# SSD mixer of an encoder kernel: accumulators emptied ahead of the weight splits, a new order at the mixer's two ends, its last two output units by token tile

## The chip, the cores and the metric

One core of one Trainium2 chip runs the whole kernel in one launch. The metric is the device time in microseconds (us). The kernel before takes 1647.73 us, the median of 3 runs (1646.65 to 1647.95).

## The reference

Four encoder layers on 256 tokens of width 1024, float32. Layers 0 and 3 have a bidirectional Mamba-2 mixer (SSD), layer 1 a gated short convolution, layer 2 a neighbourhood attention; a squared-ReLU MLP follows each, and each sub-layer ends in a layer norm. The SSD mixer:

```python
def ssd_mixer(x, w_in, conv_w, conv_b, dt_bias, a_log, d_skip, norm_w, w_out):
    zxbcdt = x @ w_in
    ...
    xbc = jax.nn.silu(depthwise_conv(xbc, conv_w) + conv_b)
    ...
    dt = jax.nn.softplus(dt_raw.reshape(bsz, seq, 2, SSD_HEADS) + dt_bias)
    y_fwd = run_ssd(xs, dt[:, :, 0], a_coef[0], bm, cm)
    y_bwd = flip(run_ssd(flip(xs), flip(dt[:, :, 1]), a_coef[1], flip(bm), flip(cm)))
    y = y_fwd + y_bwd + d_skip[:, None] * xs
    y = y.reshape(bsz, seq, SSD_D_INNER) * jax.nn.silu(z)
    return grouped_rmsnorm(y, norm_w) @ w_out
...
for i in range(DEPTH):
    ...
    x = layer_norm(alpha * x + h, ln_mix_g[i], ln_mix_b[i])
    x = layer_norm(alpha * x + sq_relu_mlp(x, ffn_w_in[i], ffn_w_out[i]), ln_ffn_g[i], ln_ffn_b[i])
```

`run_ssd` works in two chunks of 128 tokens: products within a chunk under a decay, and a state that one chunk passes to the other (the cross-chunk product).

## The kernel before

The weights come as units of 128 x 2048 float32 (1 MB). The list `units` (`plan_units`, L64) numbers them in the order of use. SyncE loads unit u into one of 3 buffers `raw` as soon as unit u-3 is split (L342). A split makes two fp32r halves: ScalarE writes `w_high` (L997), and then VectorE writes `w_low` = raw - w_high (L1338), into one of 4 slots. The slot is free when TensorE has used unit u-4 (semaphore `w_used`). TensorE multiplies three times per product (high by high, high by low, low by high).

Every engine runs its program in the order in which `build` issues it and waits on semaphores. Where a split stands in it is set by `split_to(u)`, which issues all splits up to unit u that are not issued yet. `result` is at L1000 on ScalarE and L1341 on VectorE:

```python
            def result(u):

                split_to(u + 3)
                act.wait_ge(w_used, u + 1)
                return acc_of[u]
```

So whoever empties the accumulator of unit u first splits unit u+3.

An SSD mixer has 8 groups g. Each has the units `z` (gate), `bc` (B and C), `x` and `so` (a slice of the output matrix); before them comes `dt`. The order of units is dt, z0, bc0, x0, z1, bc1, x1, z2, bc2, x2, so0, z3, bc3, x3, so1, ... z6, bc6, x6, so4, bc7, x7, z7, so5, so6, so7. TensorE's program for one step i (L848 to L858) is

- `project` z i (`tokens`, L570), then `state_products(i-1)` (L800, reads `bc` after its silu) and `turn_xs(i-1)` (L789, four transposes of `x` after its silu);
- `project` bc i (`features`, L557), `cross_chunk(i-1)` (L811) and `scan(i-1)` (L824);
- `project` x i (L557), `out_unit` so i-2 (L681, into the four banks `Y`), `turn_gated(i-1)` (L835, transposes of the gated and normalised output).

The products of L789, L800, L811, L824 and L835 share two PSUM banks `inner` in turn (`inner_bank`, L530): each waits until the one two places before it has been read. The bank of `turn_gated(g)` is read by ScalarE's `gated_high` (L1148) and then VectorE's `gated_low` (L1488), which write the operand `opT` of the output unit.

ScalarE and VectorE share the rest of a group. `start_conv` (L1062, L1068) copies the accumulator into a padded buffer and does the first tap, `taps` (L1468) on VectorE the other four; `conv_tanh` (L1076) and `silu_bc`, `silu_x`, `silu_z` (L1480) make the silu. `shift_decays` (L1091), `decays` (L1101), `join_decays` (L1498, a predicated copy) and `decayed_products` (L1508 to L1522) make the operand of `scan`. `copy_cross` (L1112) and `copy_xs` (L1121) empty the banks of L800 and L789. GpSimd scales the copied `x` twice (L432) and loads the next decays (L427). `add_cross` (L1532, L1537) and `gate_scan` (L1548, L1550) add up and gate; `squares` (L1130), a power on GpSimd (L459, L460) and `normalise` (L1138) make the grouped norm.

At the start of a mixer `time_constants` works on `dt`, and the cumulative sums go by TensorE (L771), a VectorE copy (L1594), TensorE again (`cumsum_rows`, L779) and DRAM. At its end `tail` (L699) does the last output unit by token tile, so that the layer norm of tile 0 (`norm`, L1356) can start while TensorE multiplies tile 1; the feed-forward begins with the transposes of L647 and three units of L570.

## Time and profile before

| | |
|---|---|
| profiled execution, its own time | 1646.52 us |
| its span | 1644.6 us |
| mean granted TensorE clock | 0.946 |
| TensorE matmul busy | 1491.3 us (91%) |
| TensorE weight load busy | 1379.9 us (84%) |
| VectorE busy | 991.2 us (60%) |
| ScalarE busy | 767.6 us (47%) |
| GpSimd busy | 163.9 us (10%) |
| chain that ended last | PE 66%, DVE 18%, issue 8%, ACT 7%, DMA 1% |
| DMA | 266.98 MB, mean 162 GB/s |

PE, PEld, DVE, ACT, POOL and SP are TensorE's matmuls, its weight loads, VectorE, ScalarE, GpSimd and SyncE. The granted clock is given as a share of full speed; the two levels are 0.50 (1.2 GHz) and 1.00 (2.4 GHz), and a mean between them is a share of time at each. The first mixer lies between 20 and 330 us, the second between 1142 and 1447 us. A row of the profile that reads "[4.20 <-DVE opT L1488]" says that the engine stood idle for 4.20 us before this instruction until the VectorE instruction of line 1488 on the tile opT had ended. Matmuls overlap in their records, so the time that one block takes is read from its start to the start of the next.

### The profile page before, as it was taken

The page shows a single profiled execution, that of the slowest core. Times are in us where ns is not written, and L with a number is a line of the kernel's source. Part 1 is how long each engine was busy: PE and PEld are TensorE (multiplying, and loading weights), DVE is VectorE, ACT ScalarE, POOL GpSimd, SP SyncE. Part 2 cuts the span into 40 slices and gives each one's busy share as a digit, 9 for nine tenths or more (in the row PEclk, how much of TensorE's full clock was granted, in tenths as well). Part 3 has the DMA queues.
Part 4 walks back from the last instruction along what each step waited for, and adds up shares of the span by engine and source line. Part 5 has one row for each costly group of instructions (what it writes and reads, how often), then busy time and mean ns, then how long its engine had stood idle before and what let it go on. Part 6 is the DMA issues. An engine that isn't in the chain of part 4 may idle for free.

```text
span 1644.6 us, 24792 instructions
## 1 busy us (share of the span) xinstructions
PE 1491.3 (91%) x9837; PEld 1379.9 (84%) x9837; DVE 991.2 (60%) x1227; ACT 767.6 (47%) x1103; POOL 163.9 (10%) x245
## 2 busy tenths in 40 slices
PE   6888887799999999999999999999878787799996
PEld 6877887599998999999899799998878787689995
DVE  4767766655456666555754465556776776665554
ACT  3666655344433434443355444433656664435441
POOL 1111110052231000000000000000111120000000
PEclk9899898899999999999999999999999988899998
DMA  7635543346674564555553345555644462336551
GB/s 220 183 126 154 172 138 127 102 147 200 207 218 156 188 210 143 187 195 205 170 171 121 102 138 183 194 203 151 190 152 132 152 179 103 122 110 205 205 179 52
DMA packets 198193, 266.98 MB, mean 162 GB/s; under 512 B 11768, under 2 KB 167824, under 8 KB 198080
## 3 DMA queue, kind: packets, MB, share of 16 engines
q1 hardware_dynamic: 188032, 237.53, 43.6%
q0 software_dynamic: 9200, 27.55, 6.3%
q8 instruction: 79, 1.29, 0.3%
q10 hardware_dynamic: 848, 0.32, 0.1%
q14 instruction: 34, 0.28, 0.1%
HBM read 264.19 MB, written 1.18 MB: 161 GB/s over the span
## 4 chain that ended last, share of the span: by engine, by line
PE 66%; DVE 18%; issue 8%; ACT 7%; DMA 1%; SPq 0%; DVEq 0%; POOL 0%; ACTq 0%
PE acc L557 31%; PE y L681 24%; DVE conv L1468 6%; DVE w_low L1338 6%; PE acc L570 4%; ACT w_high L997 3%; PE y L570 1%; PE inner L789 1%; DMA raw<-in_ssd_w_in 1%; PE inner L811 1%; DVE opT L1488 1%; DVE gate L1550 1%; DVE gate L1548 1%; DVE E L1532 1%; ACT square L1130 1%
## 5 line engine op out<-in xcount | busy, mean ns | idle before, releaser
L557 PE MATMUL acc<-xT,w_high 128*128 128x256 f32 (+1 forms) x3392 | 646.2, 292 | 2.7 <-DVE xT L1399 1.1
L1338 DVE TENSOR_TENSOR w_low<-raw,w_high 128x2048 fp32r<-128x2048 f32 (+1 forms) x226 | 513.1, 2275 | 175.3 <-ACT w_high L997 93.3
L557 PEld LDWEIGHTS acc<-xT,w_high 128*128 128x128 f32 x3392 | 557.3, 201 | 7.8 <-issue 3.5
L997 ACT ACTIVATE w_high<-raw 128x2048 fp32r<-128x2048 f32 (+1 forms) x226 | 428.1, 1898 | 204.5 <-PE y L681 75.4
L557 PE MATMUL acc<-xT,w_low 128*128 128x256 f32 (+1 forms) x1696 | 492.8, 291 | 0.0
L681 PE MATMUL y<-w_high,opT 128*128 128x512 f32 x1408 | 404.3, 397 | 7.9 <-DVE opT L1488 6.0
L557 PEld LDWEIGHTS acc<-xT,w_low 128*128 128x128 f32 x1696 | 339.9, 200 | 0.0
L681 PEld LDWEIGHTS y<-w_high,opT 128*128 128x128 f32 x1408 | 263.9, 191 | 61.4 <-issue 9.5
L681 PE MATMUL y<-w_low,opT 128*128 128x512 f32 x704 | 226.3, 396 | 0.0
L570 PE MATMUL acc<-w_high,xT 128*128 128x256 f32 (+1 forms) x960 | 188.5, 298 | 15.6 <-DVE xT L1399 9.3
L1354 DVE TENSOR_TENSOR opT<-conv,opT 128x512 fp32r<-128x512 f32 x56 | 39.0, 696 | 267.2 <-issue 236.6
L570 PEld LDWEIGHTS acc<-w_high,xT 128*128 128x128 f32 x960 | 160.3, 205 | 19.4 <-issue 16.0
L681 PEld LDWEIGHTS y<-w_low,opT 128*128 128x128 f32 x704 | 134.5, 191 | 29.0
L570 PE MATMUL acc<-w_low,xT 128*128 128x256 f32 (+1 forms) x480 | 141.5, 295 | 0.0
L1468 DVE SCALAR_TENSOR_TENSOR conv<-conv_pad,ssd_par,conv 128x256 f32<-128x256 f32 x256 | 104.1, 479 | 3.4 <-ACT conv L1068 3.4
L1037 ACT ACTIVATE conv<-acc 128x512 f32<-128x512 f32 x60 | 35.8, 597 | 149.3 <-PE acc L557 135.1
L409 POOL TENSOR_TENSOR small<-small,minus_half 128x1 f32<-128x1 f32 x16 | 15.9, 993 | 842.6 <-DVE small L1375 842.6
L570 PEld LDWEIGHTS acc<-w_low,xT 128*128 128x128 f32 x480 | 98.7, 206 | 0.0
L789 PE MATMUL inner<-ident,xsT 128*128 128x128 f32 x64 | 16.1, 400 | 81.0 <-DVE opT L1488 78.5
L789 PEld LDWEIGHTS inner<-ident,xsT 128*128 128x128 f32 x64 | 10.6, 202 | 87.1 <-issue 68.0
L1076 ACT ACTIVATE tanh<-conv 128x512 f32<-128x512 f32 x32 | 20.2, 631 | 135.4 <-DVE conv L1468 135.4
L1024 ACT ACTIVATE xT<-inner 128x512 fp32r<-128x512 f32 x32 | 18.1, 595 | 117.5 <-PE inner L647 117.1
(182 smaller groups left out, 1175.6 us busy)
## 6 DMA issues: line engine op xcount, KB each, us to landing
raw<-in_ffn_w_in SPq DMA_DIRECT2D x128, 512.0 KB, 4.6
raw<-in_ffn_w_out SPq DMA_DIRECT2D x128, 512.0 KB, 4.4
raw<-in_ssd_w_in SPq DMA_DIRECT2D x96, 512.0 KB, 5.1
E<-cumsum_dram POOLq DMA_DIRECT2D x32, 512.0 KB, 5.5
raw<-in_ssd_w_out SPq DMA_DIRECT2D x32, 512.0 KB, 5.8
raw<-in_sc_w_in SPq DMA_DIRECT2D x24, 512.0 KB, 4.6
raw<-in_na_w_qkv SPq DMA_DIRECT2D x24, 512.0 KB, 4.6
raw<-in_sc_w_out SPq DMA_DIRECT2D x8, 512.0 KB, 4.4
```

Of the source, the lines that this page charges most:

```text
L557: mm = nc.tensor.matmul(bank[:, c * SEQ:(c + 1) * SEQ][:, span], w[:, col:col + P], xT[:, k, low, span], start=(k == 0 and part == 0), sto ...
L570: mm = nc.tensor.matmul(bank[:, t * width:(t + 1) * width], xT[:, k, low, t * P:(t + 1) * P], w[:, k * width:(k + 1) * width], start=(k == ...
L681: mm = nc.tensor.matmul(Y[t][c][:, :], opT[:, o % ACTS, low, k, t * P:(t + 1) * P], w[:, k * D + c * 512:k * D + (c + 1) * 512], start=(fi ...
L789: mm = nc.tensor.transpose(bank[:, t * GW + c * P:t * GW + (c + 1) * P], xsT[:, m % 2, c, t * P:(t + 1) * P], ident[:, :])
L811: mm = nc.tensor.matmul(bank[:, t * GW:(t + 1) * GW], cross[m % 2][:, (1 - t) * P:(2 - t) * P], xs_end[:, (1 - t) * GW:(2 - t) * GW], star ...
L997: nc.scalar.activation(w_high[:, u % SPLIT, 0:k * c], raw[:, u % RAW, 0:k * c], ACT.Copy).then_inc(w_high_done, 1)
L1024: nc.scalar.activation(xT[:, 4 * half:4 * half + 4, 0, t * P:(t + 1) * P], bank[:, :].rearrange("p (k c) -> p k c", k=4), ACT.Copy).then_i ...
L1037: nc.scalar.activation(conv[:, o % 2, :, :], views(bank[:, :]), ACT.Relu).then_inc(relu_done, 1)
L1076: nc.scalar.activation(th[:, m % 2, :], src, ACT.Tanh, scale=scale).then_inc(tanh_done, 1)
L1338: V.tensor_tensor(w_low[:, u % SPLIT, 0:k * c], raw[:, u % RAW, 0:k * c], f(w_high[:, u % SPLIT, 0:k * c]), ALU.subtract).then_inc(w_low_d ...
L1354: V.tensor_tensor(low, src, high, ALU.subtract).then_inc(op_low, 1)
L1468: ins = V.scalar_tensor_tensor(out=y, in0=pad[:, c % 2, i, q:q + SEQ], scalar=tap(j, q, ct), in1=y, op0=ALU.mult, op1=ALU.add)
```

## The change

It keeps every instruction and moves many. On ScalarE and VectorE the mixer no longer uses `result` but `finished`, which only waits for the accumulator; the split of unit u+4 is issued by an explicit `split_to` after the accumulator of unit u has been emptied and, in a step, after the short work that others wait for. In the first step `turn_gated(0)` moves behind the projection of z 2. The last step runs bc 7, x 7, z 7 in another order against the scans; `turn_gated(6)`, the halves of so 5 and the transposes change places; and so 6 and so 7 are done together by `tail`, token tile 0 of both and then tile 1 of both.

```diff
@@ TensorE
-            def tail(s, us, first=False):
+            def tail(s, us, first=False, between=None):
...
                             mm = out_part(s, u, o + i, first and i == 0, False, [t])
+                            if between and t == 0:
+                                between()
...
-                    for i in range(1, G):
-                        if i < G - 1:
-                            project(names[("z", i)], range(NT))
+                    for i in range(1, G - 1):
+                        project(names[("z", i)], range(NT))
+                        if i == 2:
+                            turn_gated(0)
                         state_products(i - 1)
                         turn_xs(i - 1)
                         project(names[("bc", i)], range(NT))
                         cross_chunk(i - 1)
                         scan(i - 1)
                         project(names[("x", i)], range(NT))
-                        if i < G - 1:
-                            if i >= 2:
-                                out_unit(s, names[("so", i - 2)], first=(i == 2))
+                        if i >= 2:
+                            out_unit(s, names[("so", i - 2)], first=(i == 2))
                             turn_gated(i - 1)
+                    project(names[("bc", G - 1)], range(NT))
+                    state_products(G - 2)
+                    turn_xs(G - 2)
+                    project(names[("x", G - 1)], range(NT))
+                    cross_chunk(G - 2)
+                    scan(G - 2)
                     project(names[("z", G - 1)], range(NT))
-                    turn_gated(G - 2)
                     state_products(G - 1)
+                    turn_xs(G - 1)
...
                     out_part(s, names[("so", G - 3)], o, False, False, [0])
-                    turn_xs(G - 1)
-                    out_part(s, names[("so", G - 3)], o, False, False, [1]).then_inc(w_used, 1)
+                    turn_gated(G - 2)
                     cross_chunk(G - 1)
                     scan(G - 1)
-                    out_unit(s, names[("so", G - 2)], between=lambda: turn_gated(G - 1))
-                    tail(s, [names[("so", G - 1)]])
+                    out_part(s, names[("so", G - 3)], o, False, False, [1]).then_inc(w_used, 1)
+                    tail(s, [names[("so", G - 2)], names[("so", G - 1)]], between=lambda: turn_gated(G - 1))
@@ ScalarE (VectorE the same)
+            def finished(u):
                 act.wait_ge(w_used, u + 1)
                 return acc_of[u]
+
+            def result(u):
+
+                split_to(u + 3)
+                return finished(u)
@@ ScalarE, the mixer
+                    split_to(names[("dt", 0)] + 4)
                     z_tanh(0)
-
-                    split_to(names[("bc", 0)] + 3)
...
                     act.dma_start(rows_dram[j], csT[:, :]).then_inc(rows_stored, 16)
+                    split_to(names[("z", 0)] + 4)
                     conv_tanh()
+                    split_to(names[("bc", 0)] + 4)
                     start_conv("x", 0)
+                    split_to(names[("x", 0)] + 4)
                     conv_tanh()
                     shift_decays(0)
                     for i in range(1, G):
...
+                            if i == 2:
+                                gated_high(0)
+                        else:
+                            start_conv("bc", i)
+                            split_to(names[("bc", i)] + 4)
                         copy_cross(i - 1)
                         copy_xs(i - 1)
+                        if i < G - 1:
+                            split_to(names[("z", i)] + 4)
                         shift_decays(i)
-                        start_conv("bc", i)
-                        conv_tanh()
+                        if i < G - 1:
+                            start_conv("bc", i)
+                            split_to(names[("bc", i)] + 4)
+                            conv_tanh()
+                        else:
+                            conv_tanh()
+                            start_conv("x", i)
                         squares(i - 1)
                         decays(i, early)
                         normalise(i - 1)
-                        start_conv("x", i)
+                        if i < G - 1:
+                            start_conv("x", i)
                         decays(i, late)
+                        split_to(names[("x", i)] + 4)
                         conv_tanh()
-                        split_to(names[("x", i)] + 4)
                         if i == G - 1:
-                            z_tanh(G - 1)
-                        gated_high(i - 1)
-                    copy_cross(G - 1)
-                    copy_xs(G - 1)
-                    split_to(names[("so", G - 1)] + 1)
+                            z_tanh(i)
+                            copy_cross(i)
+                            copy_xs(i)
+                            split_to(names[("z", i)] + 4)
+                        if i >= 2:
+                            gated_high(i - 1)
+                            split_to(names[("so", i - 2)] + 4)
                     squares(G - 1)
                     normalise(G - 1)
-                    split_to(names[("so", G - 1)] + 2)
                     gated_high(G - 1)
@@ VectorE, taps
-                        split_to(names[(kind, g)] + 3)
@@ VectorE, the mixer
+                    split_to(names[("dt", 0)] + 4)
                     silu_z(0)
-                    split_to(names[("bc", 0)] + 3)
...
+                    split_to(names[("z", 0)] + 4)
                     silu_bc(0, taps("bc", 0))
-                    silu_x(0, taps("x", 0))
+                    split_to(names[("bc", 0)] + 4)
+                    y = taps("x", 0)
+                    split_to(names[("x", 0)] + 4)
+                    silu_x(0, y)
...
+                            if i == 2:
+                                gated_low(0)
+                            decayed_products(i - 1)
+                            split_to(names[("z", i)] + 4)
+                            join_decays(i)
+                            add_cross(i - 1)
+                            y = taps("bc", i)
+                            gate_scan(i - 1)
+                            silu_bc(i, y)
+                            split_to(names[("bc", i)] + 4)
+                        else:
+                            y = taps("bc", i)
+                            decayed_products(i - 1)
+                            split_to(names[("bc", i)] + 4)
+                            silu_bc(i, y)
+                            join_decays(i)
+                            add_cross(i - 1)
+                            gate_scan(i - 1)
                         silu_x(i, taps("x", i))
-                        split_to(names[("x", i)] + 4)
                         if i == G - 1:
-                            silu_z(G - 1)
-                        gated_low(i - 1)
-                    decayed_products(G - 1)
-                    split_to(names[("so", G - 1)] + 1)
+                            silu_z(i)
+                            split_to(names[("x", i)] + 4)
+                            decayed_products(i)
+                            split_to(names[("z", i)] + 4)
+                        if i >= 2:
+                            gated_low(i - 1)
+                            if i < G - 1:
+                                split_to(names[("x", i)] + 4)
+                            split_to(names[("so", i - 2)] + 4)
+                        else:
+                            split_to(names[("x", i)] + 4)
                     add_cross(G - 1)
                     gate_scan(G - 1)
-                    split_to(names[("so", G - 1)] + 2)
                     gated_low(G - 1)
```

VectorE in a steady step of the kernel before (w_low is a split, opT<-inner the row of `gated_low`, the three rows of L1480 `silu_bc`, `silu_x` and `silu_z`):

```order
L1480 SCALAR_TENSOR_TENSOR ring_a<-tanh,conv 128x512
L1338 TENSOR_TENSOR w_low<-raw,w_high 128x2048
L1468 SCALAR_TENSOR_TENSOR conv<-conv_pad,ssd_par,conv 128x256 x8
L1480 SCALAR_TENSOR_TENSOR xsT<-tanh,conv 128x512
L1338 TENSOR_TENSOR w_low<-raw,w_high 128x2048
L1488 SCALAR_TENSOR_TENSOR opT<-inner,ssd_par,opT 128x256 x2
L1338 TENSOR_TENSOR w_low<-raw,w_high 128x2048
L1480 SCALAR_TENSOR_TENSOR ring_c<-tanh,acc 128x512
```

and of the change (the same lines are now L1508, L1364, L1496 and L1516):

```order
L1508 SCALAR_TENSOR_TENSOR ring_a<-tanh,conv 128x512
L1364 TENSOR_TENSOR w_low<-raw,w_high 128x2048
L1496 SCALAR_TENSOR_TENSOR conv<-conv_pad,ssd_par,conv 128x256 x8
L1508 SCALAR_TENSOR_TENSOR xsT<-tanh,conv 128x512
L1516 SCALAR_TENSOR_TENSOR opT<-inner,ssd_par,opT 128x256 x2
L1364 TENSOR_TENSOR w_low<-raw,w_high 128x2048 x2
L1508 SCALAR_TENSOR_TENSOR ring_c<-tanh,acc 128x512
```

The split of the next `x` unit moved from ahead of `gated_low` to behind it.

VectorE at the start of a mixer in the kernel before, from the copy of the cumulative sums' rows (L1603) to `silu_x(0)`:

```order
L1603 COPY cumsum_rows<-inner 64x256
L1468 SCALAR_TENSOR_TENSOR conv<-conv_pad,ssd_par,conv 128x256 x8
L1480 SCALAR_TENSOR_TENSOR ring_a<-tanh,conv 128x512
L1338 TENSOR_TENSOR w_low<-raw,w_high 128x2048
L1468 SCALAR_TENSOR_TENSOR conv<-conv_pad,ssd_par,conv 128x256 x8
L1480 SCALAR_TENSOR_TENSOR xsT<-tanh,conv 128x512
```

and of the change:

```order
L1631 COPY cumsum_rows<-inner 64x256
L1364 TENSOR_TENSOR w_low<-raw,w_high 128x2048
L1496 SCALAR_TENSOR_TENSOR conv<-conv_pad,ssd_par,conv 128x256 x8
L1508 SCALAR_TENSOR_TENSOR ring_a<-tanh,conv 128x512
L1364 TENSOR_TENSOR w_low<-raw,w_high 128x2048
L1496 SCALAR_TENSOR_TENSOR conv<-conv_pad,ssd_par,conv 128x256 x8
L1364 TENSOR_TENSOR w_low<-raw,w_high 128x2048
L1508 SCALAR_TENSOR_TENSOR xsT<-tanh,conv 128x512
```

Three splits stand in this stretch where one stood: the first came from ahead of the sums, the last from behind `silu_x(0)`.

VectorE at the end of a mixer of the change, from `silu_z(7)` (ring_c) to `gated_low(7)`, the last row:

```order
L1508 SCALAR_TENSOR_TENSOR ring_c<-tanh,acc 128x512
L1364 TENSOR_TENSOR w_low<-raw,w_high 128x2048
L1536 TENSOR_TENSOR E<-E,inner 128x1024
L1540 SCALAR_TENSOR_TENSOR E,small<-inner,ident 128x128 x2
L1550 SCALAR_TENSOR_TENSOR own_token<-dts,small,skip 128x4 x2
L1364 TENSOR_TENSOR w_low<-raw,w_high 128x2048
L1516 SCALAR_TENSOR_TENSOR opT<-inner,ssd_par,opT 128x256 x2
L1364 TENSOR_TENSOR w_low<-raw,w_high 128x2048
L1560 TENSOR_TENSOR E<-inner,decay_from_end 128x512
L1565 TENSOR_TENSOR E<-E,ring_b 128x512
L1576 TENSOR_TENSOR gate<-E,inner 128x512
L1578 SCALAR_TENSOR_TENSOR gate<-gate,ring_c 128x512
```

The three splits are so 7 and the feed-forward's units 0 and 1. Before, unit 0 stood there too, ahead of `add_cross(7)`, and unit 1 between `gate_scan(7)` and `gated_low(7)`; now unit 1 stands ahead of `add_cross(7)`.

## Rows read from the trace of the kernel before

**Rows 1.** TensorE's waits, second mixer: waited for, us in total, times, longest

```profile
PE inner L789 <- DVE opT L1488: 38.5, 7, 9.9
PE inner L835 <- ACT gate L1138: 5.3, 2, 4.9
PE inner L779 <- DVE cumsum L1594: 3.3, 1, 3.3
```

**Rows 2.** Stretches: length, busy of PE, PEld, DVE, ACT, POOL, clock, DMA share, GB/s

```profile
1222.61:1358.35 135.74, 118.93 (x803) 112.75 (x802) 95.83 (x148) 81.07 (x156) 21.12 (x24) 0.90 0.51 156
106.33:242.17 135.84, 119.06 (x803) 112.89 (x802) 95.73 (x148) 81.06 (x156) 21.13 (x24) 0.90 0.51 155
1248.65:1252.65 4.00, 4.00 (x21) 4.00 (x20) 3.93 (x10) 3.62 (x10) 1.16 (x1) 0.50 1.10 305
```

**Rows 3.** Timeline around one wait of L789: start us, us, engine, line, operation

```profile
1276.44 1.89 ACT L997 ACTIVATE w_high<-raw 128x2048 fp32r<-128x2048 f32 x1
1276.65 0.69 DVE L1480 SCALAR_TENSOR_TENSOR xsT<-tanh,conv 128x512 f32<-128x512 f32 x1 [0.77 <-ACT tanh L1076]
1278.24 0.82 ACT L1148 ACTIVATE opT<-inner,ssd_par 128x256 fp32r<-128x256 f32 x2
1278.43 2.29 DVE L1338 TENSOR_TENSOR w_low<-raw,w_high 128x2048 fp32r<-128x2048 f32 x1 [1.09 <-ACT w_high L997]
1280.63 0.87 DVE L1488 SCALAR_TENSOR_TENSOR opT<-inner,ssd_par,opT 128x256 fp32r<-128x256 f32 x2
1281.65 1.08 PE L789 MATMUL inner<-ident,xsT 128*128 128x128 f32 x4 [4.20 <-DVE opT L1488]
```

**Rows 4.** Timeline of TensorE, block starts in the same step

```profile
1290.28 0.60 PE L811 MATMUL inner<-ring_a,E 128*128 128x256 f32 x2
1292.85 0.48 PE L557 MATMUL acc<-xT,w_high 128*128 128x256 f32 x2
1298.68 0.63 PE L681 MATMUL y<-w_high,opT 128*128 128x512 f32 x2
1304.15 0.60 PE L835 MATMUL inner<-ident,gate 128*128 128x128 f32 x4
```

**Rows 5.** Groups of lines in steady steps: xcount | busy us, mean ns | idle before

```profile
L1338 DVE TENSOR_TENSOR w_low<-raw,w_high 128x2048 fp32r<-128x2048 f32 x16 | 36.6, 2288 | 21.4 <-issue 17.0 <-ACT w_high L997 4.3
L1498 DVE COPY_PREDICATED E<-suffix,E 128x1024 f32<-128x1024 uint32 x4 | 5.4, 1356 | 0.0
L1508 DVE TENSOR_TENSOR E<-E,inner 128x1024 f32<-128x1024 f32 x4 | 4.9, 1215 | 0.0
L432 POOL TENSOR_TENSOR ring_b<-ring_b,own_token 128x512 f32<-128x512 f32 x1 | 2.1, 2052 | 1.8 <-DVE own_token L1522 1.8
L432 POOL TENSOR_TENSOR ring_a<-ring_b,decay_to_end 128x512 f32<-128x512 f32 x8 | 8.8, 1101 | 125.6 <-ACT ring_b L1121 111.3 <-issue 14.3
```

**Rows 6.** Timeline of the start of the second mixer

```profile
1161.83 2.29 DVE L1338 TENSOR_TENSOR w_low<-raw,w_high 128x2048 fp32r<-128x2048 f32 x1 [0.82 <-issue]
1165.38 0.58 ACT L1062 ACTIVATE conv_pad<-acc 128x512 f32<-128x512 f32 x1
1166.49 0.58 ACT L1068 ACTIVATE conv<-conv_pad,ssd_par 128x256 f32<-128x256 f32 x1
1167.11 3.26 DVE L1468 SCALAR_TENSOR_TENSOR conv<-conv_pad,ssd_par,conv 128x256 f32<-128x256 f32 x8 [1.65 <-ACT conv L1068]
1179.91 0.66 PE L789 MATMUL inner<-ident,xsT 128*128 128x128 f32 x4 [1.34 <-DVE xsT L1480]
```

**Rows 7.** Timeline of the end of the second mixer

```profile
1427.59 0.69 DVE L1550 SCALAR_TENSOR_TENSOR gate<-gate,ring_c 128x512 f32<-128x512 f32 x1
1430.31 0.91 ACT L1138 ACTIVATE gate<-gate,small 128x256 f32<-128x256 f32 x2 [1.09 <-POOL small L460]
1446.99 0.47 PE L570 MATMUL acc<-w_high,xT 128*128 128x256 f32 x2 [0.84 <-DVE xT L1399]
```

**Rows 8.** DMA issues of the page: count, KB each, us to landing

```profile
raw<-in_ssd_w_in SPq DMA_DIRECT2D x96, 512.0 KB, 5.1
```

28 lines of the change are left out of this document (12 added, 16 removed).

## The prediction

> **What bounds the kernel now.** I read the waits of TensorE first, then stretches with granted clock, then the timelines of the places where it waits. Outside the two SSD mixers TensorE has hardly a gap. Inside the second mixer its largest wait is one line's: the transposes of `turn_xs` (L789) wait seven times, 38.5 us in all, for a VectorE row of L1488, `gated_low`; behind it come `turn_gated` (L835) and `cumsum_rows` (L779) [rows 1]. The steady part of a mixer, four steps from the cross-chunk product of group 1 to that of group 5, takes 135.74 us in the second mixer and 135.84 in the first, 34.0 a step, at a mean granted clock of 0.90 [rows 2]. So the clock is at its lower level, 1.2 GHz, part of the time: the four microseconds after one of these waits show 0.50 [rows 2].
>
> One wait in detail [rows 3]. The bank that `turn_xs` wants is the one that held the turned gate of the group before, and it comes free when `gated_low` (L1488) ends, 1281.50. That row stands behind a weight split: ScalarE splits at 1276.44 before it copies the turned gate at 1278.24, VectorE's w_low runs from 1278.43, then L1488. TensorE has nothing to do for 4.20 us. What follows is slow too: the four transposes and the `bc` projection behind them take 8.63, from 1281.65 to the next product at 1290.28; at full clock the equal `x` projection takes 5.83, and four transposes 0.4 [rows 3, 4].
>
> **The change, part by part.** No instruction is added or removed, matmuls and splits are as many; only their order changes, so each term is a shift of waits.
>
> *A steady step (groups 1 to 5).* `gated_high` and `gated_low` now run before the split of the next `x` unit instead of behind it. If TensorE never waits, a step costs the 34.0 less the wait (4.2, and 0.2 by which the next matmul overlaps the last) and less what the lower clock adds (8.63 - 6.23 = 2.4): 27.2. Does VectorE keep up? It is busy 95.83/4 = 23.96 of a step [rows 2]. I laid its chain out from the start of a cross-chunk product, with w_low at 2.2 since successive VectorE rows overlap by 0.08: `add_cross`, two 128x512 rows of 0.69, starts at 1.06 and ends at 2.45; four taps of two tiles (3.26 [rows 6]) 5.65; `gate_scan` 7.0; from its end to the end of the normalised gate 2.94 [rows 7], 9.95; pad and first tap on ScalarE 1.69 [rows 6], 11.65; taps 14.9; tanh 0.65, 15.55; `gated_high` 0.82, 16.4; `gated_low` 0.87, 17.2 [rows 3]; two w_low (2.29 [rows 5]) 21.6; `silu_z` 22.2; products 1.2 [rows 5] and small rows 0.9, 24.3; w_low 26.5; the predicated copy 1.36 [rows 5], 27.8. The next `add_cross` can start at 28.2. So the chain fits, 0.4 to spare, and what TensorE waits for (L1488 at 17.2, wanted near 21) has 4 us in hand. TensorE is the bound, at full clock: 4 x (34.0 - 27.2) = **27.2 a mixer**. The loads: 5.3 MB a step now in 27.2, 195 GB/s after 156 [rows 2]; each is issued when w_low three units earlier ends, 5.1 from issue to landing [rows 8], and in my layout each has over 4 us left.
>
> *The mixer's start* (second mixer's times). w_low of `bc` 1, which held up the cumulative sums until 1164.12 [rows 6], moves behind them: the copy of the sums is 3.0 earlier, the 3.3 wait of L779 goes [rows 1]. But three splits now stand between the sums and `silu_x(0)`, where one stood, and VectorE's w_low waits each time for ScalarE's w_high (1.89 [rows 3]), which has moved behind the pad: pad and first tap of `bc` 0 end at 1164.1, w_high 1166.0, w_low 1168.3, taps 1171.5, tanh 1172.1, w_high 1174.0, pad and tap of `x` 0 1175.7, w_low before it 1176.4, taps 1179.6, w_low of `z` 2 1181.8, `silu_x` 1182.5. `turn_xs(0)` ran at 1179.91 after 1.34 of waiting [rows 6]; now at 1182.5, after 8.2, and the clock falls: `bc` 1 ends 5.2 later than before. Then `z` 2 fills the 4.9 that `turn_gated(0)` waited [rows 1], so `z` 2 ends 4.0 earlier. The split of `so` 0 still stands ahead of `gated_low(0)`; `turn_xs(1)` runs at 1212.2, was 1214.9. At the cross-chunk product of group 1 the gain is **2.3 a mixer**, nearly nothing for so much moved.
>
> *The mixer's end*, from the cross-chunk product of group 5 (its start is 0 here). Before, the feed-forward's first matmul came at 1446.99 - 1358.35 = 88.64 [rows 2, 7]. Now `bc` 7 and `x` 7 come ahead of the work that waited 9.9. VectorE: taps of `bc` 7 end 25.2, products 27.3, w_low 29.5, `silu_bc` 30.1, predicated copy 31.5, `add_cross` 32.9, gate 34.15, taps of `x` 7 37.4; ScalarE normalises until 37.1, decays 38.4, splits `so` 7 until 40.25, tanh 40.9; `turn_xs(7)` runs at 41.6, TensorE was there at 36.5: a wait of 5.1. Half of `so` 5 at half clock until 47.4, `turn_gated(6)` 48.0. `scan(7)` wants the bank that `gated_low(6)` empties behind w_low of the feed-forward's unit 0: 49.8 to 51.6. The second half of `so` 5 ends 54.4 and only then can its slot be split again (the feed-forward's unit 1), which both engines do **ahead of** `add_cross(7)` and `squares(7)`: w_high 56.3, w_low 58.7, `add_cross` 60.1, gate 61.4, normalised 64.3 [rows 7]. TensorE has the first half of `so` 6 until 57 and then waits 7.3 for `turn_gated(7)`, 1.9 more for L1488. Three halves follow (5.47/2 each at full clock [rows 4], 8.2, and 2.1 for the clock): 77.2. The last two units by token tile cover the layer norm of tile 0, whose 1.2 wait goes; the feed-forward starts at 79.4. Gain 88.64 - 79.4 = **9.2 a mixer**.
>
> Sum: 2 x (27.2 + 2.3 + 9.2) = 77.4. From the profiled 1646.5 that gives 1569.1; the median of the runs is 1.2 higher, **1570**.
>
> *The rule that speaks against it.* GpSimd's two products of L432 have the same shape; the one on ring_a takes 1101 ns, the one on ring_b in a steady step 2052, while VectorE's w_low stays at its 2288 in the mean of sixteen [rows 5]. So where they meet it is GpSimd that is held, and it has time. In the new order L432 falls beside a w_low, a row with two SBUF inputs. The Trainium skill (SBUF — State Buffer, SBUF: two separate sides) says that VectorE with two SBUF inputs and a GpSimd operation exclude each other for a whole instruction, whichever starts first. By the rule VectorE could as well be the one that stands still; this trace shows GpSimd's side of it, 2052 against 1101, and not VectorE's. What the other side would make here is rival A.
>
> **Rivals.** *A: VectorE becomes the bound.* Two L432 in its chain, 1.1 and 1.0, make the chain 27.8 - 1.06 + 2.1 = 28.9 a step, over TensorE's 27.2 by 1.7. Four steps lose 7, of which TensorE's 4 in hand cover more than half, and the end starts late: 4 to 7 a mixer, 1578 to 1584. For it: 88% busy, 0.4 to spare. Against: w_low never differs by a GpSimd row's length in this trace.
> *B: the wait is only shortened.* ScalarE or a bank I placed too early leaves 1 to 2 us before L789, and the clock still falls after each: a step saves 3, not 6.8, 30 less in all: 1600. Against: 4 us in hand.
> *C: slower, the loads.* The splits of `x` and `so` are now back to back, so loads are issued in bursts. If two of four loads of each step landed a load's 5.1 [rows 8] late on VectorE's chain, a step would take 37.4, 3.4 over now, 27 for eight steps; less the 23 won at both ends: 1651. It decides once a step loses over 9.7. Against: 4 us of room at the tightest.
> *D: nothing changes.* The split could have been no cause, another bank release being as late: 1647. Against: [rows 3] show w_low alone between the copy and L1488.
> The start and end may also miss: if `turn_xs(0)` or the end of the mixer were no better than now, 2.3 + 9.2 a mixer fall away, 1593; if VectorE and ScalarE hide the long waits there, each wait is worth 5 to 7, 1556.
>
> **How the numbers follow.** Forecast 0.70, A 0.14, B 0.11, C 0.02, D 0.03. The range takes A and the misses at the ends, from 1556 to 1593; B, C and D stay out. About 0.2% is what a measurement of this kernel tells from no change. Faster 0.96, same 0.02, slower 0.02.
>
> **What would show it.** Right: 108 to 110 us between the cross-chunk products of groups 1 and 5 at granted clock 1.00, no L789 wait in the steady steps; two waits of 5 to 9 us left at the start (L789), one of 5 before `turn_xs(7)` and one of 7 before `turn_gated(7)`. Wrong: VectorE without gaps in the steady steps and its `add_cross` later after each product (A); L789 still waiting (B); w_high waiting for raw (C).

## The result, and the profile after

The changed kernel takes 1594.41 us, the median of 4 runs (1592.47 to 1595.0), beside 1647.76 for the kernel before (1646.65 to 1647.95): a ratio of 0.9676, 95% interval 0.9659 to 0.9692. The forecast was 1570 with a range up to 1593. The profiled run took 1592.47 with a span of 1590.6, so 54.0 of span went where 77.4 were forecast.

TensorE's waits in the second mixer, answering to [rows 1] (line, what it waited for: us in all, times, longest):

```profile
PE inner L791 <- DVE xsT L1508: 10.9, 2, 8.1
PE inner L837 <- ACT gate L1148: 10.2, 4, 7.5
PE inner L791 <- DVE opT L1516: 7.4, 1, 7.4
PE inner L813 <- DVE E L1540: 4.4, 4, 3.6
```

L789 is now L791 and L1488 is L1516. The seven waits of 38.5 us for `gated_low` have become one, at the start. The steady steps have no L791 wait, as forecast. The waits for the normalised gate (L837 on L1148) have grown from 5.3 us to 10.2, and waits for a bank that VectorE empties late (L813) are new.

Four steps from the product of group 1 to that of group 5, in the first mixer and in the second, and last the end of the second mixer up to the feed-forward's first matmul (us, busy time of PE, PEld, DVE, ACT, POOL, granted clock, DMA share, GB/s), answering to [rows 2]:

```profile
104.81:217.27 112.46, 109.91 (x802) 103.17 (x801) 93.99 (x145) 81.56 (x157) 34.86 (x23) 1.00 0.55 175
1194.69:1307.17 112.48, 109.89 (x803) 103.16 (x801) 94.02 (x145) 81.49 (x157) 34.82 (x23) 1.00 0.55 177
1307.17:1394.17 87.00, 67.45 (x385) 59.50 (x385) 59.86 (x93) 39.87 (x79) 18.76 (x14) 0.86 0.36 122
```

The clock is up, at 1.00. But 112.5 is not the 108.8 of the forecast: the four steps of the second mixer are 27.12, 27.45, 28.95 and 28.96. And the end takes 87.00, hardly less than the 88.64 before, where 79.4 was forecast.

One late step on GpSimd, ScalarE and VectorE shows where the time goes (start us, us, engine, line):

```profile
1278.54 3.03 POOL L432 TENSOR_TENSOR ring_b<-ring_b,own_token 128x512 f32<-128x512 f32 x1 [1.84 <-DVE own_token L1550]
1281.51 1.15 POOL L427 DMA_DIRECT2D E<-cumsum_dram  x2
1289.59 1.82 POOL L459 TENSOR_SCALAR small<-small 128x2 f32<-128x2 f32 x1 [6.92 <-ACT square L1140]
1291.49 0.71 POOL L460 TENSOR_TENSOR small<-small,minus_half 128x2 f32<-128x2 f32 x1
```

```profile
1292.23 0.91 ACT L1148 ACTIVATE gate<-gate,small 128x256 f32<-128x256 f32 x2 [1.57 <-POOL small L460]
```

```profile
1278.37 2.29 DVE L1364 TENSOR_TENSOR w_low<-raw,w_high 128x2048 fp32r<-128x2048 f32 x1
1280.58 2.19 DVE L1526 COPY_PREDICATED E<-suffix,E 128x1024 f32<-128x1024 uint32 x1
...
1287.86 0.69 DVE L1578 SCALAR_TENSOR_TENSOR gate<-gate,ring_c 128x512 f32<-128x512 f32 x1
1288.47 0.69 DVE L1508 SCALAR_TENSOR_TENSOR ring_a<-tanh,conv 128x512 f32<-128x512 f32 x1
1289.07 2.28 DVE L1364 TENSOR_TENSOR w_low<-raw,w_high 128x2048 fp32r<-128x2048 f32 x1
1294.79 3.26 DVE L1496 SCALAR_TENSOR_TENSOR conv<-conv_pad,ssd_par,conv 128x256 f32<-128x256 f32 x8 [3.43 <-ACT conv L1078]
```

L459 works on 128x2 elements and still takes 1.82 us: it ends at 1291.41, when w_low (L1364) has ended at 1291.35. ScalarE's normalise (L1148) waits for it and ends at 1293.14, 4.59 after the gate (L1578 ended at 1288.55), not 2.94; the pads of `x` follow, and VectorE idles 3.43 before its taps. L432 begins under a w_low and ends at 1281.57, 0.99 after VectorE has started its next row, the predicated copy (L1526). That row stands still meanwhile: it takes 2.19 us, where it took 1356 ns in the mean [rows 5]. As groups over the four steps (xcount | busy us, mean ns), after, and below them L459 of the kernel before in its own four steps:

```profile
L1526 DVE COPY_PREDICATED E<-suffix,E 128x1024 f32<-128x1024 uint32 x3 | 6.6, 2188 | 0.0
...
L432 POOL TENSOR_TENSOR ring_a<-ring_b,decay_to_end 128x512 f32<-128x512 f32 x4 | 11.1, 2778 | 42.7 <-ACT ring_b L1131 42.7
L432 POOL TENSOR_TENSOR ring_b<-ring_b,own_token 128x512 f32<-128x512 f32 x3 | 9.1, 3026 | 5.5 <-DVE own_token L1550 5.5
L459 POOL TENSOR_SCALAR small<-small 128x2 f32<-128x2 f32 x4 | 7.3, 1817 | 23.3 <-ACT square L1140 23.3
```

```profile
L459 POOL TENSOR_SCALAR small<-small 128x2 f32<-128x2 f32 x4 | 0.8, 193 | 24.0 <-ACT square L1130 24.0
```

Nothing was added to GpSimd. Its busy time in four steps grew from 21.12 us to 34.82 [rows 2], and the rows that grew are those that meet a w_low.

### The profile page after: what moved, and what is told of

It is laid out like the page before. It is cut to its first block, busy times and chain, and to the rows that moved or that the text cites. A ratio compares the mean times of both kernels' runs of the same rounds, so it can differ in the third digit from the quotient of the medians.

```text
span 1590.6 us, 24788 instructions
## 1 busy us (share of the span) xinstructions
PE 1470.5 (92%) x9837; PEld 1357.3 (85%) x9837; DVE 997.9 (63%) x1227; ACT 769.1 (48%) x1103; POOL 212.5 (13%) x245
## 4 chain that ended last, share of the span: by engine, by line
PE 63%; DVE 21%; ACT 7%; issue 6%; POOL 2%; DMA 1%; SPq 0%; DVEq 0%; ACTq 0%; POOLq 0%
PE acc L557 28%; PE y L681 26%; DVE w_low L1364 6%; DVE conv L1496 6%; PE acc L570 4%; ACT w_high L1004 2%; POOL small L459 1%; DVE E L1526 1%; ACT square L1140 1%; PE y L570 1%; DVE E L1536 1%; DMA raw<-in_ssd_w_in 1%; POOL small L460 1%; DVE gate L1578 1%; DVE E L1565 1%
## 5 line engine op out<-in xcount | busy, mean ns | idle before, releaser
L557 PE MATMUL acc<-xT,w_high 128*128 128x256 f32 (+1 forms) x3392 | 625.2, 286 | 2.7 <-DVE xT L1428 1.1
L1364 DVE TENSOR_TENSOR w_low<-raw,w_high 128x2048 fp32r<-128x2048 f32 (+1 forms) x226 | 514.5, 2284 | 110.1 <-ACT w_high L1004 82.0
L557 PEld LDWEIGHTS acc<-xT,w_high 128*128 128x128 f32 x3392 | 538.8, 195 | 7.8 <-issue 3.5
L557 PE MATMUL acc<-xT,w_low 128*128 128x256 f32 (+1 forms) x1696 | 483.5, 285 | 0.0
L557 PEld LDWEIGHTS acc<-xT,w_low 128*128 128x128 f32 x1696 | 329.5, 194 | 0.0
L1496 DVE SCALAR_TENSOR_TENSOR conv<-conv_pad,ssd_par,conv 128x256 f32<-128x256 f32 x256 | 105.7, 485 | 41.2 <-ACT conv L1078 41.2
L432 POOL TENSOR_TENSOR ring_a<-ring_b,decay_to_end 128x512 f32<-128x512 f32 x16 | 33.2, 2075 | 187.7 <-ACT ring_b L1131 169.0
L496 POOL DMA_DIRECT2D E<-in_na_rpb x64 | 34.1, 538 | 92.4 <-ACT conv L1047 91.3
```

Source lines behind the costliest of these rows:

```text
L432: return nc.gpsimd.tensor_tensor(spread(dst, shape), spread(tri_b[:, n % 2, :], shape), factors, ALU.mult)
L496: pool.dma_start(dst, src).then_inc(window_landed[h % WINDOW_BUFS], 16)
L557: mm = nc.tensor.matmul(bank[:, c * SEQ:(c + 1) * SEQ][:, span], w[:, col:col + P], xT[:, k, low, span], start=(k == 0 and part == 0), sto ...
L1364: V.tensor_tensor(w_low[:, u % SPLIT, 0:k * c], raw[:, u % RAW, 0:k * c], f(w_high[:, u % SPLIT, 0:k * c]), ALU.subtract).then_inc(w_low_d ...
L1496: ins = V.scalar_tensor_tensor(out=y, in0=pad[:, c % 2, i, q:q + SEQ], scalar=tap(j, q, ct), in1=y, op0=ALU.mult, op1=ALU.add)
```

## The experiments

All times below are medians, with the ratio to the kernel before run beside them. The stretches are read from one profiled run of each kernel, from the first matmul of each cross-chunk product and of the feed-forward (us, first mixer / second mixer). "between" is from the feed-forward behind the first mixer to group 0's product of the second, so it holds the start of the second mixer too:

```text
kernel              group 0-1      groups 1-5       5 to feed-fwd   between  span
before              34.91/34.37    135.84/135.74    88.67/88.64     857.4    1644.6
changed             32.61/31.14    112.46/112.48    86.75/87.00     859.5    1590.6
e1 mean square      28.58/30.21    108.48/108.48    80.38/81.37     868.5    1578.1
e2 own sliver       31.10/31.16    109.93/109.97    87.02/84.88     859.8    1583.7
e3 both             30.18/28.69    108.48/108.48    80.21/79.69     858.6    1562.5
e4 undo x+4         33.32/31.80    120.14/118.74    84.82/85.73     859.7    1605.4
e9 undo bc+4        33.09/31.60    116.85/115.80    88.32/89.71     859.8    1607.1
e13 undo both       33.77/33.74    121.97/123.45    87.36/87.25     868.4    1627.3
e14 undo z+4 too    33.78/34.32    135.35/136.08    87.69/87.72     868.3    1654.5
e5 start            30.48/30.37    112.48/112.45    88.69/86.97     854.0    1581.0
e6 end              32.61/31.16    112.51/112.45    76.09/79.10     859.7    1574.3
e7 late turn        28.93/27.88    109.71/109.68    82.37/81.95     859.6    1570.4
e8 all three        27.98/27.07    113.13/113.14    74.66/74.66     853.7    1548.4
e11 late and end    27.60/27.73    109.72/109.68    73.08/71.47     861.4    1552.5
```

### Is it GpSimd? (e1, e2, e3)

e1 moves the scale of the mean square from GpSimd to VectorE, with a reciprocal in place of the power, so it leaves out that part of the output:

```diff
                             silu_bc(i, y)
+                            rms(i - 1)
                             split_to(names[("bc", i)] + 4)
 ...
-                        rms_power(g)
```

> GpSimd's two small operations per group (the scale 1/sqrt of the mean square) are done by VectorE behind silu_bc instead, and GpSimd's are dropped; the power is replaced by a reciprocal, so this part of the output is not computed. Theory 1 (GpSimd's small operation waits for the end of w_low, 1.82 us instead of 0.19, and so delays normalise, the pads of x, and VectorE itself): the steady step falls from 28.95 us to about 27.3, PE's wait ahead of turn_gated (0.9) goes, the idle time of VectorE ahead of taps x falls from 3.4 to about 1.7, total about 1594 - 2 x 5.5 x 1.6 = 1576 us. Theory 2 (VectorE's own work with ScalarE's chain is 29 us long and GpSimd's stretch is only a by-product with slack): step 28.9, total 1592 to 1597.

Measured: 1577.53 us (1575.76 to 1579.8), ratio 0.9576 [0.956, 0.9592]. Four steps with the end behind them, second mixer:

```profile
1191.77:1300.25 108.48, 108.48 (x803) 103.40 (x802) 98.19 (x156) 81.82 (x156) 20.18 (x16) 1.00 0.61 189
1300.25:1381.62 81.37, 64.15 (x387) 56.83 (x385) 57.34 (x96) 39.85 (x79) 12.11 (x8) 0.87 0.36 118
```

Every step is 27.12 and TensorE is busy for all of 108.48; VectorE is busier than before (98.19 after 94.02) and yet in time. The end is 5.6 shorter too (6.4 in the first mixer): it starts in time, and it is rid of an L459 of 1.82 of its own. That the median fits the expected number so well is partly luck: the mixers and what lies ahead of them gave 21.5 of span, and "between" took 9.0 more (see the last group).

e2 leaves GpSimd's second product a sliver of two columns:

```diff
-                        times_heads(xs_own, n, spread(own_token[:, n % 2, 0, :],
-                                                      [[HPG, NT], [1, HPG], [0, HD]])).then_inc(xs_skip, 1)
+                            nc.gpsimd.tensor_tensor(xs_own[:, 0:2], tri_b[:, n % 2, 0:2],
+                                                    own_token[:, n % 2, 0, 0:2], ALU.mult).then_inc(xs_skip, 1)
```

> GpSimd's product ring_b (1.04 us of its own) is shrunk to a sliver in groups 1 to 7, so the token's own term is left out there. Theory 1 (each of GpSimd's operations excludes VectorE's sbuf-to-sbuf ones): COPY_PREDICATED returns from 2.19 us to 1.36 and the step is 0.8 us shorter (28.1), total about 1585. Theory 2 (predicated copy is slow for another reason, its operands or ScalarE): it stays at 2.2 and the total at 1594.

Measured: 1585.88 us (1584.69 to 1597.39), ratio 0.9646 [0.9612, 0.968]; the last full steps are 28.14. VectorE's predicated copy in the four steps:

```profile
L1530 DVE COPY_PREDICATED E<-suffix,E 128x1024 f32<-128x1024 uint32 x3 | 4.0, 1349 | 0.0
```

It is back at 1349 ns with unchanged operands: what held it was L432.

> Both edits of the two kernels before. Theory 1: VectorE is rid of GpSimd save for one product a group, and PE sets the step, 27.1 us, as was forecast for the change; total about 1572. Theory 2: 1592 to 1597.

Measured: 1567.96 us (1564.21 to 1569.38), ratio 0.9518 [0.9503, 0.9533]. With both collisions away the stretches are what the forecast had: 108.48 for four steps (forecast 108.8), 80.21 and 79.69 for the end (forecast 79.4). Theory 2 fell in all three.

### What gave the 23 us of a mixer's steps? (e4, e9, e13, e14)

The prediction named one move, the gated operand ahead of the split of x+4. e4 takes that back (VectorE; ScalarE's tanh goes ahead of the split again as well):

```diff
-                            gated_low(i - 1)
-                            if i < G - 1:
-                                split_to(names[("x", i)] + 4)
+                        split_to(names[("x", i)] + 4)
+                        if i >= 2:
+                            gated_low(i - 1)
```

> Only the order in steps 2 to 6 (and the last) is taken back: the split x+4 stands ahead of the gated operand on both engines, everything else as changed. If this one move makes the shorter step, the step returns to about 33.9 us and the total to about 1594 + 2 x 4.5 x 4.9 = 1638. If the rest of the change (accumulators emptied before splits) gives half of it, the step is 31 and the total about 1615.

Measured: 1607.33 us (1604.38 to 1607.43), ratio 0.9756 [0.9742, 0.9771]. Both numbers were missed: four steps cost 7.7 and 6.3 more, not 20. The L791 waits are back in the second mixer's four steps, but with 8.0 us in all, the longest 2.8. e9 puts w_high of bc+4 back on ScalarE between normalise and the pads of `x`:

```diff
                             start_conv("bc", i)
-                            split_to(names[("bc", i)] + 4)
                             conv_tanh()
 ...
+                            split_to(names[("bc", i)] + 4)
                             start_conv("x", i)
```

> The changed kernel with one thing taken back on ScalarE alone: in steps 1 to 6 w_high of the unit bc+4 is made where it was before, between normalise and the pads of x, instead of ahead of the tanh of bc. VectorE's order is untouched. Theory 1 (the chain gate, normalise, pads of x, taps x sets the changed step, so what is put in it costs its full length): w_high's 1.9 us is added, step 28.95 to about 30.8, and the total 1594 + 2 x 5.5 x 1.9 less what the first steps have in hand, about 1610. Theory 2 (the chain has slack, since VectorE waits for GpSimd elsewhere anyway): 1594 to 1598.

Measured: 1608.51 us (1607.31 to 1609.52), ratio 0.9751 [0.9716, 0.9786]. Four steps 4.4 and 3.3 longer, the end 1.6 and 2.7: theory 1's total, though the late steps went to 29.8 and 30.9 unevenly.

> The changed kernel with the x+4 split ahead of the gated operand again (both engines) and w_high of bc+4 between normalise and the pads of x again (ScalarE). Theory 1 (the parts have separate prices that add, 13 and 14 us): 1621. Theory 2 (each is covered in part by what the others leave: whichever wait is removed, the next split in the chain takes its place, so only together do they give the whole): 1630 or more, steps of 32 to 34 us.

Measured: 1628.85 us (1628.5 to 1629.54), ratio 0.9876 [0.9846, 0.9906]. The median lies by theory 2's number, the stretches speak for theory 1: four steps cost 9.5 and 11.0 more than in the changed kernel, where the separate prices add to 12.1 and 9.6. The rest of the median is "between", 8.8 longer. e14 also puts the split of z+4 back (VectorE; ScalarE's goes back behind `shift_decays`):

```diff
-                            split_to(names[("z", i)] + 4)
                             join_decays(i)
                             add_cross(i - 1)
+                            split_to(names[("z", i)] + 4)
```

> As the kernel before, and the split of z+4 back behind shift_decays on ScalarE and behind add_cross on VectorE: a step's order as before, the ends as changed. Theory: steps 2 to 6 take 33.9 to 34.1 us again and the total is 1647 less what the ends gave, 4 to 8 us: 1639 to 1643. If a step stays below 33 something else in the change (PE's order, the so split) has a share that I haven't named.

Measured: 1655.71 us (1653.84 to 1657.33, 10 runs), ratio 1.0039 [1.0023, 1.0054]. The steps are back at 34.0 with four L791 waits of 4.19, as before. So of the 23 us of a mixer's four steps in the second mixer, the x+4 order carries 6.3, bc+4 with it 11.0, and z+4 the other 12.6, taken back in this order; z+4 was not taken back alone. The expected total was missed by 13: slower than the kernel before, although its steps are within 0.5 of before's and its ends (87.7) 0.9 shorter. The table puts the difference in "between": 868.3, where the kernel before has 857.4 and the changed one 859.5.

### Mending what was found (e7, e6, e5, e8, e11, e12, e15)

e7 leaves GpSimd alone, but takes what is urgent from behind it: TensorE turns the gated operand in the middle of the next z unit, and ScalarE makes the pads of `x` before it normalises.

```diff
-                        project(names[("z", i)], range(NT))
+                        zb = project(names[("z", i)], [0])
+                        if i >= 2:
+                            turn_gated(i - 2)
+                        project(names[("z", i)], [1], zb)
 ...
                         decays(i, early)
-                        normalise(i - 1)
                         if i < G - 1:
                             start_conv("x", i)
+                        normalise(i - 1)
```

> The changed kernel, whole computation, GpSimd's work left as it is, but nothing urgent hangs on it any more: the gated operand is turned in the middle of the next z projection, and ScalarE makes x's pads before it normalises. Theory 1 (GpSimd's blocked operation costs only because pads of x and turn_gated stand behind normalise): the step falls from 28.95 us to 27.1 to 27.5 though GpSimd's small operation stays long (1.8 us or more), total about 1578. Rival (the exclusion slows VectorE itself, which has no slack whatever the order): step 28.1 or more, total 1585 or more.

Measured: 1573.72 us (1572.3 to 1575.32), ratio 0.9555 [0.9539, 0.9571]. Steps of 27.42, and L459 is as slow as ever:

```profile
L459 POOL TENSOR_SCALAR small<-small 128x2 f32<-128x2 f32 x4 | 7.3, 1818 | 15.2 <-ACT square L1143 15.2
L432 POOL TENSOR_TENSOR ring_b<-ring_b,own_token 128x512 f32<-128x512 f32 x4 | 4.2, 1046 | 0.9 <-DVE own_token L1555 0.9
```

L459's collision stays, and TensorE waits for nothing in these steps (busy for 109.19 of 109.68); they are 0.3 each over e1's 27.12. But L432 no longer meets a w_low, which the edit brought along unasked: it takes 1.05, and the predicated copy 1.31. So e7 shows that L459's collision can be hidden, not that both can, and it doesn't tell the late turn from the early pads. It fits theory 1 in the step and is 4 better than its total.

e6 is about the wait of 7.5 before `turn_gated(7)`. Here are ScalarE and VectorE ahead of it in the changed kernel:

```profile
1369.26 1.92 ACT L1004 ACTIVATE w_high<-raw 128x2048 fp32r<-128x2048 f32 x1 [8.18 <-PE y L681]
```

```profile
1371.26 2.29 DVE L1364 TENSOR_TENSOR w_low<-raw,w_high 128x2048 fp32r<-128x2048 f32 x1 [8.61 <-ACT w_high L1004]
1373.47 0.68 DVE L1560 TENSOR_TENSOR E<-inner,decay_from_end 128x512 f32<-128x512 f32 x1
```

Both engines idle over 8 us because a split for the feed-forward waits for TensorE to be done with a slot, and `add_cross(7)` (L1560) is queued behind. The edit (VectorE the same):

```diff
-                        if i >= 2:
+                        if 2 <= i < G - 1:
                             split_to(names[("so", i - 2)] + 4)
```

> The changed kernel, whole computation, without the split of the feed-forward layer's first unit in the last step (it is made behind gated_low(7) then). Theory 1 (the wait of 7.5 us before turn_gated(7) is this split, which waits for PE to be done with output unit 5 and holds add_cross(7) and gate_scan(7) on VectorE behind it): the wait falls to 0 to 1 us, total about 1594 - 2 x 7 = 1580. Theory 2 (the wait is the length of the chain scan, gate, mean square, normalise, as the prediction held): it stays at 7 or more, total 1592 to 1595, or more if the split is then late for the next layer.

Measured: 1575.99 us (1574.16 to 1576.89), ratio 0.9565 [0.955, 0.9579]. The wait is gone and the end stretches are 10.7 and 7.9 shorter. The stretch of the second mixer:

```profile
1298.73:1377.83 79.10, 66.98 (x384) 59.32 (x385) 59.79 (x93) 39.76 (x79) 18.77 (x14) 0.89 0.39 134
```

e5 orders the start anew (ScalarE, then VectorE; what is moved leaves its old place, and ScalarE's `gated_high(0)` goes ahead of z 2 too):

```diff
                     z_tanh(0)
+                    split_to(names[("z", 0)] + 4)
 ...
-                    y = taps("x", 0)
-                    split_to(names[("x", 0)] + 4)
-                    silu_x(0, y)
+                    silu_x(0, taps("x", 0))
 ...
+                            if i == 2:
+                                gated_low(0)
                             silu_z(i)
+                            if i <= 2:
+                                split_to(names[("x", i - 1)] + 4)
```

> The changed kernel, whole computation, with the mixer's start ordered anew. ScalarE makes w_high(z0+4) right behind z_tanh(0), in time it idles; VectorE makes w_low(x0+4) and w_low(x1+4) behind silu_z of the next step, and both engines serve the gated operand of group 0 ahead of z 2. Theory 1 (the waits before turn_xs(0) and turn_xs(1) come from weight splits that stand ahead of the taps, of silu_x and of gated_low(0), not from VectorE's amount of work): the first wait falls from 8.1 us to about 5.6, the second from 7.4 to about 4, so 4 to 6 us a mixer, total 1582 to 1586. Theory 2 (VectorE has so much to do between bc 0 and x 1 that only the place of the wait moves): sum of the two waits stays within 1 us, total 1592 to 1595.

Measured: 1589.79 us (1582.93 to 1591.15), ratio 0.9641 [0.9619, 0.9663]. In the profiled run the two waits of TensorE in the second mixer are 3.1 and 5.8 instead of 8.1 and 7.4, 6.6 less together, as theory 1 has it, and the span is 9.6 less. But 3.0 of that lie ahead of group 0's product of the first mixer, where two executions of the changed kernel itself differ by 2.5 (72.20 and 74.70, the second from e16), and this execution is the lowest of four. The median, 4.6 less, lies between the two theories; e18 below repeats it.

> The three edits of the kernels before together, whole computation. If their parts add: 1594 less about 16 (late turn), 10 (start) and 14 (end) = about 1554 us. If the shorter start and the late turn gain the same waits: 1562.

Measured: 1550.38 us (1546.74 to 1553.24), ratio 0.9409 [0.9393, 0.9425]. The parts add: by their medians e7, e6 and e5 gave 20.7, 18.4 and 4.6, which makes 1550.7. Repeated on another chip:

> The kernel with the late turn, the mended start and the mended end, once more, in five rounds: 1547 to 1553 us, 0.941 of the kernel before.

Measured: 1557.31 us (1545.6 to 1563.4), ratio 0.9434 [0.9401, 0.9467]: above the expected range, with the mixers' stretches the same to 0.1 us and 863.8 between them in the profiled run. By either median it is faster than e5, e6 and e7. Without the start's edit:

> The late turn and the mended end together, start as changed. If the start is worth in this company what its two waits promise (5 to 7 us a mixer less), this kernel is 10 to 13 us above the one with all three edits, 1560 to 1563; if the start's gain only moves, 1552 to 1555.

Measured: 1553.09 us (1551.46 to 1564.94), ratio 0.9431 [0.9383, 0.948]. Not told apart from e8 and e15. The stretches show why so little is left: at group 1's product of the first mixer e8 is 7.2 ahead (95.56 after 102.77), e15, the same kernel, 4.1 (98.68). Then both give 3.4 back in the steps (113.13 after 109.72) and 1.6 at the end (74.66 after 73.08); in the second mixer the end gives back 3.2. I take it that VectorE still has the w_low rows to do that were put off; no run separates that. What is left of the start's gain in this company is not told from nothing.

e12 tries one more thing in the last step:

```diff
                             silu_bc(i, y)
+                            silu_x(i, taps("x", i))
                             join_decays(i)
                             add_cross(i - 1)
                             gate_scan(i - 1)
-                        silu_x(i, taps("x", i))
```

> All three edits, and in the last step VectorE and ScalarE serve x 7 (taps, tanh, silu) ahead of the decays of group 7 and the gate of group 6. TensorE waited 5.9 us for x 7 there. If that wait is the queue ahead of taps x and not the chain of x 7 itself, it falls to about 1, and the gate of group 6, 4 us later, is still in time for turn_gated(6): 1550 - 2 x 4.5 = 1541. Rival (the gate of group 6, the decays and the products of group 7 come late instead, and the wait reappears before turn_gated(6) or scan(7)): 1548 to 1552.

Measured: 1564.89 us (1557.78 to 1572.68), ratio 0.9473 [0.9427, 0.9519]; the ends take 78.02 and 80.89 instead of 74.66. The rival won, and its price was larger than it said:

```profile
PE inner L837 <- DVE E L1547: 6.9, 1, 6.9
```

The wait of 5.9 before `turn_xs(7)` came back as one of 6.9 before `turn_gated(6)`.

### The last two units, and the clock between the mixers (e10, e16, e17, e18)

```diff
-                    tail(s, [names[("so", G - 2)], names[("so", G - 1)]], between=lambda: turn_gated(G - 1))
+                    out_unit(s, names[("so", G - 2)], between=lambda: turn_gated(G - 1))
+                    tail(s, [names[("so", G - 1)]])
```

> The changed kernel with TensorE's last two output units whole, one after the other, as before (turn_gated(7) inside unit 6's last quarter), instead of by token tile; VectorE and ScalarE untouched. Theory 1 (by token tile the layer norm of tile 0 is covered by matmuls, and the late turn costs nothing): the wait before turn_gated(7) shrinks from 7.5 us to about 2, but TensorE then waits 3 to 5 us more for the normed tile; about 1594 + 2 x 2 = 1598. Rival (the longer cover ahead of turn_gated(7) is worth more than the covered norm): below 1592.

Measured: 1599.19 us (1591.0 to 1600.8), ratio 0.9685 [0.9643, 0.9727]. In the profile (the 1591.0 run) the ends are 2.8 and 1.1 shorter than by token tile, against theory 1: TensorE's wait before `turn_gated(7)` fell to 6.1 only, but its wait for the normed tile is 1.2 and not 3 to 5. The median is 5 longer, against the rival. The next three repeat the changed kernel, the whole units and e5's start beside each other:

> The changed kernel itself, five rounds, beside the next two: 1592 to 1596 us when the clock between the mixers stays up (mean granted clock 0.962), some 8 to 10 more in executions where it falls once in the layers between the mixers.

> Last two output units whole again. If its times are of two kinds, about 1591 and about 1600, and the changed kernel's too, the part is worth nothing that can be told; if only this kernel's are, the whole units cost 5 us by what they do to the clock of the layers behind.

> The start's edit alone. Executions of two kinds, about 1582 and about 1590, by the clock between the mixers; the lower kind 10 us under the changed kernel's lower kind.

Measured: the changed kernel 1593.98 us (1592.19 to 1594.68), ratio 0.9662 [0.9637, 0.9687]; whole units 1599.14 (1598.67 to 1600.24), ratio 0.9695 [0.9671, 0.972]; the start's edit 1591.06 (1586.53 to 1594.11), ratio 0.9642 [0.9614, 0.967]. The changed kernel did as expected. The start's edit missed both of its numbers, 1582 and 10 less: its lowest is 1586.53, 5.7 below the changed kernel's lowest, so that e5's 1582.93 is one execution in nine and the edit is worth 3 to 5 us by the medians. e17's profiled run again has shorter ends (83.80 and 85.94), and 868.8 between the mixers where the changed kernel has 859.1. Of eight executions of the whole units seven lie between 1598.67 and 1600.8 and one at 1591.0; the changed kernel's eight lie between 1592.19 and 1595.0. So the 5 us lie outside the mixer that was edited. The place can be seen in two runs of one and the same kernel, the one with all three edits: e15, then e8, each from 1.3 us behind the same wait in a feed-forward layer:

```profile
486.50:491.50 5.00, 5.00 (x28) 5.00 (x28) 4.49 (x2) 1.88 (x2) 0.00 (x0) 0.56 0.24 76
491.50:501.50 10.00, 10.00 (x49) 10.00 (x49) 2.29 (x1) 2.40 (x2) 0.00 (x0) 0.50 0.67 218
501.50:509.00 7.50, 7.50 (x42) 7.50 (x42) 4.78 (x8) 1.92 (x1) 0.00 (x0) 0.60 0.23 80
```

```profile
481.60:486.60 5.00, 5.00 (x47) 5.00 (x46) 4.49 (x2) 2.64 (x4) 0.00 (x0) 1.00 0.24 76
486.60:496.60 10.00, 10.00 (x88) 10.00 (x88) 7.38 (x9) 3.63 (x2) 0.00 (x0) 1.00 0.84 278
496.60:504.10 7.50, 7.50 (x65) 7.50 (x64) 0.74 (x2) 3.18 (x4) 0.00 (x0) 1.00 0.42 142
```

In both TensorE had waited 1.07 us for the layer norm (L557 on L1433). In e15 it then ran at 1.2 GHz for some 20 us (28 and 49 matmuls in the first 5 and the next 10 us, where e8 did 47 and 88) and was 10 us later; in e8 it stayed at 2.4 GHz. What decides between the two is open. e1, e12, e13, e14, e15, e17 and e18 had the low stretch in their profiled runs, the changed kernel in neither of its two.

## Why the prediction missed

- **The wait, and what the change does to it: right.** The steps have no L791 wait and run at clock 1.00. TensorE is the bound once GpSimd's collisions are away (e3: 108.48; forecast 108.8); in the changed kernel itself the chain through VectorE is, from the third of the four steps on.
- **"From its end to the end of the normalised gate 2.94": the step that failed.** It was read in the kernel before at the mixer's last group [rows 7], where no w_low runs beside L459. In the new order L459 falls under w_low of bc+4 in each steady step, and the term is 4.59. The predicated copy takes 2.19 for 1.36. Together the chain is 2.5 longer where I had "0.4 to spare". Steps: 23.4 and 23.3 a mixer, not 27.2.
- **The mixer's end: 1.9 and 1.6, not 9.2**, the largest miss. Its layout began with a VectorE in time and had the taps of `bc` 7 end 25.2 after group 5's product. They ended 30.54 after it in the changed kernel and 25.28 after it in e1, both counted from the products at 1307.17 and 1300.25:

```profile
1333.67 4.04 DVE L1496 SCALAR_TENSOR_TENSOR conv<-conv_pad,ssd_par,conv 128x256 f32<-128x256 f32 x8
```

```profile
1322.27 3.26 DVE L1495 SCALAR_TENSOR_TENSOR conv<-conv_pad,ssd_par,conv 128x256 f32<-128x256 f32 x8
```

VectorE came late by what the steps had lost, and lost more in step 6, where L459 and L432 (beside these taps) collide again: 32.35 us between the products of groups 5 and 6, 27.12 in e1. e1 gives back 6.4 and 5.6 of the 7.3 and 7.6 missing. The wait before `turn_gated(7)` was 7.49, forecast 7.3, with the cause named: a split waiting for its slot. What I didn't draw from it is that making this split later is free (e6).
- **The mixer's start: 1.5 and 1.1, not 2.3.** The same kernel in e16 has -1.0 and 1.5, so the first mixer's figure is not told from what varies ahead of it. The first wait was 8.1 (forecast 8.2). The second was 7.4. The prediction's own times give 5.6 for it: `turn_xs(1)` at 1212.2, and TensorE 4.0 ahead of the 1210.58 at which it stood ready before. The chain to `gated_low(0)` has the same 1.6 behind L459 (the wait is 5.7 in e1).
- **Rival A** had the step's number (28.9; measured 28.95) and half of its mechanism: I let both products of L432 hold VectorE, 2.1 in all, and missed that tiny L459 holds ScalarE, and ScalarE VectorE. One product costs the copy 0.83 and L459 1.65, so that the number fits so closely is luck. A had 4 to 7 a mixer for the steps and the late end together, hence 1578 to 1584; they cost 11.1 and 11.5. I gave it 0.14, arguing that w_low never differs by a GpSimd row's length [rows 5]. That showed who waits when w_low came first, not that waiting is harmless.
- **The page's rule** (the Trainium skill, SBUF — State Buffer, SBUF: two separate sides: two SBUF inputs on VectorE and a GpSimd operation that reads SBUF exclude each other for a whole instruction, whichever starts first): the traces agree, in both directions. L459 waits out w_low, 1.82 for 0.19. And in e1, where L432 starts 0.10 ahead of w_low, w_low takes 3.09 for 2.29:

```profile
1159.63 1.05 POOL L432 TENSOR_TENSOR ring_b<-ring_b,own_token 128x512 f32<-128x512 f32 x1 [0.61 <-DVE own_token L1549]
```

```profile
1159.73 3.09 DVE L1363 TENSOR_TENSOR w_low<-raw,w_high 128x2048 fp32r<-128x2048 f32 x1 [0.18 <-issue]
```

- **"`gated_high` and `gated_low` now run before the split" as the reason of the step:** too narrow. Taken back alone, that order costs 6.3 of 23 (e4); the w_high of bc+4 and the place of z+4's split carry the rest (e13, e14). The number didn't suffer, since I laid out the whole new order.
- **Rivals B, C, D** did not occur: no L791 wait in the steady steps, and no split waits for a load there. (The prediction's "faster 0.96, same 0.02" should have been 0.95 and 0.03 by its own rivals.)

The sum, by span: 2.0 missing at the starts, 7.8 in the steps, 14.8 at the ends, less 1.2 gained behind the second mixer, make the 23.4 between 77.4 and 54.0.

## What to carry to other kernels

When a change moves work on VectorE, lay GpSimd's operations over the new order too, one by one, however small: an operation of 0.19 us whose result ScalarE waits for took 1.82 here, until the VectorE row of 2.28 that it landed under had ended. If such a collision can't be avoided, put nothing urgent behind it (e7 got steps of 27.42 with L459's collision in place). And a split for the next layer that waits for a slot doesn't belong ahead of the last work of this one.

## What I hadn't expected of the hardware

One program has executions that differ by 10 us through a single stretch of 20 us at half clock, some 200 us behind the mixer that was edited, after a wait of 1.07 us that in other executions is followed by no such stretch (e15 and e8). e1's and e13's profiled runs have it too, and it made their medians fit an expectation that the stretches don't bear out in detail. Compare stretches of the timeline, and only then totals.
